# Two feed-forwards opened in another order: block sums ahead of scaled blocks, the seventh operand's low part last

## What is computed

```python
# first block
h2 = rmsnorm(x, norm_ffn[l])
gate, up = jnp.split(h2 @ w_ffn_in[l], 2, axis=-1)
x = x + (jax.nn.silu(gate) * up) @ w_ffn_out[l]
...
# second block
m = rmsnorm_2(x, norm_pre_mlp[l])
y = jnp.square(jax.nn.relu(m @ w_up[l])) @ w_down[l]
x = x + rmsnorm_2(y, norm_post_mlp[l])
```

## Time and profile before

| what | us |
|---|---|
| median of 3 runs | 2688.08 (2687.24 to 2689.71) |
| the profiled execution, its own time | 2686.19 |
| its span | 2684.5 |
| TensorE busy | 2594.2 (97%) |
| VectorE busy | 1859.6 (69%) |
| GpSimd busy | 1222.8 (46%) |
| ScalarE busy | 1042.5 (39%) |

### The profile page before, as it was taken

How to read it: one execution, slowest core, us unless ns; L and a number is a source line. 1 busy time by engine, 2 the same in 40 slices (tenths; PEclk the granted TensorE clock), 3 DMA queues, 4 the chain that set the end, 5 groups by cost and what they waited for, 6 DMA issues and landing times.

```text
span 2684.5 us, 32398 instructions
## 1 busy us (share of the span) xinstructions
PE 2594.2 (97%) x12362; PEld 2088.1 (78%) x12362; DVE 1859.6 (69%) x2107; ACT 1042.5 (39%) x1446; POOL 1222.8 (46%) x763
## 2 busy tenths in 40 slices
PE   7999999999999999999998999989898999999998
PEld 5888787887787888887786788656786888877777
DVE  7565665457658666668879647766558666778887
ACT  5223343323224333334435111656555433434444
POOL 2222222223447888884333443241135888723331
PEclk9999999999999999999999999999999999999999
DMA  5333333244342434245641442401333554754443
GB/s 193 118 103 114 122 94 126 79 157 145 129 145 61 118 102 118 76 133 200 223 130 55 142 149 98 122 1 46 128 85 95 164 160 142 225 158 159 159 141 142
DMA packets 335840, 339.49 MB, mean 126 GB/s; under 512 B 19723, under 2 KB 254838, under 8 KB 335686
## 3 DMA queue, kind: packets, MB, share of 16 engines
q1 hardware_dynamic: 329446, 313.81, 37.2%
q10 hardware_dynamic: 6240, 23.59, 2.2%
HBM read 228.55 MB, written 107.77 MB: 125 GB/s over the span
## 4 chain that ended last, share of the span: by engine, by line
PE 54%; DVE 9%; issue 2%; DMA 2%; ACT 1%; POOL 0%; SPq 0%; DVEq 0%; ACTq 0%; POOLq 0%
PE ps L3729 37%; PE ps L567 9%; PE ps L2787 2%; DVE op_lo L3806 2%; PE ps L2810 1%; PE ps L2797 1%; DVE sw_lo L3625 1%; PE ps L3291 1%; DVE acc L4052 1%; DVE acc L4059 1%; DMA x_block<-acc 0%; DVE acc L2313 0%; DMA acc<-x_feature_major 0%; DVE x L2734 0%; DMA op_raw<-hidden 0%
## 5 line engine op out<-in xcount | busy, mean ns | idle before, releaser
L3729 PE MATMUL ps<-op_hi,sw_hi 128*128 128x512 f32 x1765 | 690.3, 391 | 16.4 <-DVE op_lo L3806 6.5
L3729 PE MATMUL ps<-op_hi,sw_lo 128*128 128x512 f32 x1765 | 686.9, 389 | 0.0
L3729 PE MATMUL ps<-op_lo,sw_hi 128*128 128x512 f32 x1765 | 686.8, 389 | 0.0
L3729 PEld LDWEIGHTS ps<-op_hi,sw_hi 128*128 128x128 f32 x1765 | 331.3, 188 | 97.6 <-issue 16.5
L3729 PEld LDWEIGHTS ps<-op_hi,sw_lo 128*128 128x128 f32 x1765 | 331.3, 188 | 69.5
L3729 PEld LDWEIGHTS ps<-op_lo,sw_hi 128*128 128x128 f32 x1765 | 331.4, 188 | 67.7 <-issue 0.5
L533 POOL TENSOR_TENSOR w_hi_t<-w_raw,ones 128x1024 fp32r<-128x1024 f32 (+1 forms) x60 | 116.1, 1940 | 532.7 <-DMA w_raw<-in_w_in 238.7
L3615 ACT ACTIVATE sw_hi<-sw_sumNone 128x512 fp32r<-128x512 f32 (+1 forms) x252 | 157.0, 624 | 329.6 <-PE ps L3729 237.8
L3625 POOL TENSOR_TENSOR sw_lo<-sw_sumNone,sw_hi 128x512 fp32r<-128x512 f32 x138 | 215.0, 1568 | 33.2 <-ACT sw_hi L3615 33.1
L3576 POOL TENSOR_TENSOR sw_sumNone<-sw_raw 128x512 f32<-128x512 f32 (+1 forms) x63 | 114.2, 1813 | 225.6 <-DVE sw_lo L3625 204.1
L3615 ACT ACTIVATE sw_hi<-sw_raw 128x512 fp32r<-128x512 f32 (+1 forms) x188 | 116.8, 622 | 199.6 <-PE ps L3729 198.3
(11 more groups left out here) (502 smaller groups left out, 5433.2 us busy)
## 6 DMA issues: line engine op xcount, KB each, us to landing
op_raw<-hidden SPq DMA_DIRECT2D x42, 1024.0 KB, 8.8
w_raw<-in_w_in SPq DMA_DIRECT2D x47, 512.0 KB, 4.6
sw_raw<-in_w_ffn_in SPq DMA_DIRECT2D x44, 512.0 KB, 5.1
hidden<-hidden_blocks SPq DMA_DIRECT2D x13, 1536.0 KB, 6.1
hidden<-hidden_blocks SPq DMA_DIRECT2D x14, 1280.0 KB, 5.0
sw_raw<-in_w_up SPq DMA_DIRECT2D x32, 512.0 KB, 8.4
sw_raw<-in_w_down SPq DMA_DIRECT2D x32, 512.0 KB, 5.5
acc<-proj SPq DMA_DIRECT2D x30, 512.0 KB, 4.5
```

The costliest lines, as they stand in the source:

```text
L3729: mm = pe.matmul(out, w, x[:, k, :], start=(k == 0 and i == 0 and r < 4), stop=(k == n - 1 and i == 2), skip_group_check=r >= 4)
```

## The change

In the first opening, DVE makes y_lo of tile 0 only, then the sum "22" of pair 0, then the other three y_lo, then u3 and "22" of pair 1, and only then the scaled blocks; `gate_post` and `up_post` no longer make these two sums. `product` lets (0,6) wait for y_lo tile by tile. In the second opening, operand 6 is parted last instead of first: ACT's high parts go 1, 2, 3, 5, 6, DVE makes the low part of 1 where that of 6 was, and that of 6 behind u3 of pair P2+1.

```diff
-PARTED = (6, 1, 2, 3, 5)
+PARTED = (1, 2, 3, 5, 6)
...
-POSTS = [(0, "u2"), (1, "u2"), (0, "u3"), (0, "22"), (1, "u3")]
-POSTS += [(p, what) for p in range(2) for what in OUTS_OF_PAIR[2 + (p == 0):]]
+POSTS = [(0, "u2"), (1, "u2"), (0, "u3"), (0, "22"), (1, "u3"), (1, "22")]
+POSTS += [(p, what) for p in range(2) for what in OUTS_OF_PAIR[3:]]
...
 # gate_post
-            post_sum(dve, p, what, hidden(i, n))
+            if (p, what) != (0, "22"):
+                post_sum(dve, p, what, hidden(i, n))
...
 # up_post
-            post_sum(dve, p, what, hidden(i, x))
+            if (p, what) != (1, "22"):
+                post_sum(dve, p, what, hidden(i, x))
...
 # f1_dve
-            for k in range(4):
+            y_lo(dve, 0)
+            dve.wait_ge(*count("t_lo", 16))
+            dve.wait_ge(*count("b_lo", 9))
+            post_sum(dve, 0, "22", hidden(0, 6))
+            for k in range(1, 4):
                 y_lo(dve, k)
             for k in (KT - 2, KT - 1):
                 x1_spilled(dve, k)
-            dve.wait_ge(*count("t_lo", 16))
+            post_u3(dve, 1)
             dve.wait_ge(*count("b_lo", 12))
+            post_sum(dve, 1, "22", hidden(0, 1))
             dve.wait_ge(S["rstd_ready"], NORM_AT["ffn"] + 1)
             gate_post(dve, 0, "22")
-            post_u3(dve, 1)
...
 # wo2_act
-            parted_hi(act, 6)
+            parted_hi(act, 1)
             norm_root(act, "mlp", rstd2[:, :])
...
 # product
-            operand_ready(pe, p, r)
+            if (p, r) != (0, 6):
+                operand_ready(pe, p, r)
...
             for k in range(n):
+                if (p, r) == (0, 6):
+                    pe.wait_ge(*count("b_lo", KT + k + 1))
...
 # f2_act
-            parted_hi(act, 1)
...
             parted_hi(act, 5)
+            parted_hi(act, 6)
...
 # hidden_dve
-                parted_lo(dve, 6)
+                parted_lo(dve, 1)
             next_lo(dve, p, 1)
             post_u3(dve, p)
+            if q == 1:
+                parted_lo(dve, 6)
             if q:
                 mix2_dve(dve, q - 1, (2, 3))
             else:
-                parted_lo(dve, 1)
                 dve.wait_ge(S["rstd_ready"], NORM_AT["mlp"] + 1)
```

## The result

The changed kernel takes **2691.6 us** (median of 20 runs, 2688.88 to 2694.3), the kernel before 2687.8 us beside it (20 runs): a ratio of 1.0014, 95% interval 1.0008 to 1.0021. So it is 3.8 us slower, inside the 0.2% that the forecast called no change. The forecast was 2693.3 us, its range 2689.0 to 2696.6. Its profiled execution took 2691.47 us, span 2688.5, against 2686.19 and 2684.5: 5.3 us more by its own time, 4.0 by the span.

What follows compares the result with a forecast made beforehand. TensorE, busy 97%, was taken as the bound, its waits set by VectorE's full queue and turns with GpSimd. First opening 1.1, second 1.3 and clock 2.8 summed to +5.2 us on 2688.08: 2693.3 us, range 2689.0 to 2696.6.

Steps and rivals of the forecast that it cites:

- (a): First opening: with only one y_lo ahead of pair 0's "22", (0,6) starts at 849.4, a gain of 1.4 us.
- (c): First opening: scaling of pair 0's "22" begins 2.0 us later, delaying sw_lo(13); (1,6) still starts at 856.06, gaining 2.9 us.
- (d): First opening: GpSimd's four turns of 1.7 us behind sw_lo(13) make (2,0) start at 862.9, costing +1.1 us.
- (e): Second opening: block sums and operands 2, 3, 5 move 3.4 us forward; (P2+1,3) and (P2+1,5) start sooner, 2.1 us gained.
- (f): Second opening: "22" stands behind operand 6, and VectorE waits one more GpSimd turn; (P2+1,6) comes later, costing +1.3 us.
- The clock: Behind the two new long waits, one in each opening, the granted clock falls once of the two, costing +2.8 us.
- the row of 3.94: Before 22.94 in the old profile: a 3.94 us wait, then 5.6 us of matmuls at half speed, 2.8 us lost.
- Rival B: Both openings: both new waits lower the clock, +8.0 us in all, 2696.1 us; chance 0.22.
- D: Both openings: turns with GpSimd fall out better, -0.6 and -0.5 us, no long wait, 2687.0 us; chance 0.11.
- E: Both openings: the waits simply go, GpSimd being no bound; 7.9 us gained, 2680.2 us; chance 0.05.
- C: Both openings: neither new wait lowers the clock, +2.4 us, 2690.5 us; chance 0.24.

Runs made afterwards that it cites:

- e3: The changed kernel with sw_hi(13) moved ahead of the SiLU of pair 0's "22" on ScalarE; 2686.7 us in one execution.
- e4: The changed kernel with a PSUM bank replacing one SBUF operand in the second gate scaling and gate-up products of pairs 0 and 1; 2689.9 us in one execution.
- e2: The first opening of the kernel before with the changed kernel's second opening; 2690.3 us, ratio 1.0012 to the kernel before.
- e6: The changed kernel with VectorE's "22" of pair P2+1 put ahead of operand 6's low part and other work; 2689.0 us, ratio 1.0008 to the kernel before.
- e1: The changed kernel's first opening with the second opening of the kernel before; 2690.6 us, ratio 1.0009 to the kernel before.
- e10: The kernel before with nine unread matmuls ahead of (1,6); 2684.4 us, ratio 0.9990 to the kernel before.
- e5: e3 with pair 2's weights fetched one product sooner; 2687.6 us in one execution.
- e7: e5 and e6 in one kernel; 2686.4 us, ratio 0.9998 to the kernel before.
- e9: e10 with the second opening of e6 and 12 unread matmuls ahead of (P2+2,0); 2684.5 us, ratio 0.9993 to the kernel before.
- e11: e7 with the mixes of pairs 0 and 1 behind u3 and "22" of pair 2, and 12 unread matmuls ahead of (P2+2,0); 2684.2 us, ratio 0.9991.
- e8: The changed kernel with 14 unread matmuls ahead of (2,0) and of (P2+1,6); 2686.0 us, ratio 0.9998 to the kernel before.

## Why the prediction was right

The chains of the two openings were seen rightly. That the time came within 1.7 us of the forecast is in part luck: structure and clock together came to 1.1 us more than forecast, and something that the sum did not have took 2.5 off again. By its own steps:

- **(a)** (0,6) at 849.4: measured 849.21. Its wait by tiles was used: it stood 0.43 us inside. The turns fell on y_lo(1) and (2) (3.52 us for two) and not on (2) and (3), with the same sum.
- **(c)** The scaling of "22" of pair 0 at 852.8, 2.0 us later: measured 853.06, 2.2 us. The chain behind it was as said. sw_lo(13) was put at 854.7 to 856.0, at 1.30 alone; it began at 855.01 and took 1.79, since a scaling of VectorE met it too. This is the mis-sized part: 0.8 us at the end of sw_lo(13), 856.80. (1,6), put at 856.06, started at 856.90 for it.
- **(d)** Four turns of 1.7 behind it: predicted 6.9 us, measured 856.76 to 863.54, 6.8. (2,0) at 862.9 (+1.1) was therefore 863.64, **+1.9**, beyond the end of +1.6 that was given. e3 confirms the chain, e4 the turns.
- **(e)** (P2+1,5) at +19.1 from (P2,5): measured +19.00.
- **(f)** +1.3: measured **+1.04**. The two op_lo went from 5.58 to 6.69, the 1.1 us of the one further turn. e2 shows the same alone. That VectorE's unchanged sum of work had to hold (P2+1,6) was true only of this order: e6 has it 5.5 us sooner, and the bound is then GpSimd, which (f) called no bound.
- **The clock.** +2.8 as one fall of the two: the sum is near, the mechanism not. The clock fell behind both waits, in this profile and in every other one that has them unfilled, and cost 1.7 us each time, 3.4 together, less than the 2.8 taken from the row of 3.94; only e1 paid 2.8 for one. Rival B had the number of falls right and, but for e1, their size wrong; the forecast's "one fall of the two" was wrong.
- **What the sum left out** is that the kernel it is measured against pays for its own wait of 2.3 to 2.6 us. Its profile showed 1.00 there, and was taken for the rule. Structure 1.9 + 1.0 and clock 3.4 make 6.3 us; the medians differ by 3.8. The 2.9 us that e10 takes off the kernel before, if they are all clock, bring it to 3.4; e10's interval allows 0.3 to 5. That the forecast's +5.2 is near the difference of the two profiled executions (5.3; 4.0 by the span) is chance, for the clock in stretches that no edit touches differs by as much. By the same rule, a low clock behind the wait of 2.12 us at 1716 to 1719 took 5.1 us in the profile before and 3.4 in the one after; behind one of 6.5 us at 1466 to 1469 again 5.1 and 3.4; behind one of 1.90 us at 1889 nothing before and 1.7 after. Together that is 10.2 us before and 8.5 after, though not all of it is lost time, since TensorE also rests in these stretches.
- **Rivals.** D and E fell: GpSimd's operations were all at 1.61 to 1.79, and the scaling ended at 853.74, not before 852.2. C fell, since the clock fell both times; its 2690.5 is near the median only because it leaves out both the falls and what the kernel before pays.

Open stays how often the kernel before falls at (1,6): profiles show single executions, and of the waits of 2.1 to 2.6 us here two lowered the clock (e2, e4) and four did not (before, e3, and e5 and e7 at (2,5)).

## What to carry to other kernels

Where an in-order engine is full, moving one sum forward moves a wait. Follow what the displaced operation feeds through every engine behind it, and then further than the first gain: in e5, e7, e9 and, in its second opening, e11 the gain at one product was spent waiting at the next bound (VectorE's u3; weights that landed late). Several short waits can cost less than one long one of the same sum: in these two openings the clock fell only behind waits of over 2.5 us. Where such a wait can't be removed, matmuls that nobody reads, kept shorter than the wait, kept the clock up here (e8; 4.3 us by the ratios) and moved the start behind them by 0.0 to 0.3 us. And a profile of the kernel before is one execution: read its clock at each wait as a sample.

## What the hardware showed

- In the two openings the granted clock fell behind waits of 2.85 to 3.76 us in all ten places where a profile has one; behind those of 2.1 to 2.6 us in two of six; behind those of 1.5 us and less in none. TensorE was at full work on both sides. The falls began between 1.2 us ahead of the wait's end (e1) and 0.8 us behind it (the changed kernel, second opening). Ten of the twelve cost 1.7 us each, the other two 2.8 (e1) and 2.9 (e2).
- Length alone does not settle it: elsewhere, where TensorE also rests between shorter pieces of work, the clock fell behind a wait of 2.12 us in all 14 profiles (at about 1716) and behind one of about 1.9 us in 11 of 14 (at about 1889).
- A 128x512 operation on GpSimd takes 1.27 to 1.30 us alone and 1.6 to 1.8 against a VectorE operation with two SBUF operands; a PSUM operand on VectorE's side in place of one of them takes the difference away (e4).
- e3 and e5 have the same list on VectorE, but in e5 GpSimd starts on pair 2 sooner. VectorE's u3 of pair 2 then came 28.4 us behind (0,5) (874.45 - 846.08), in e3 27.4 (873.43 - 846.07): feeding GpSimd sooner put a full VectorE 1.0 us back, which fits the turns that the two take, though no run isolates it.
- The releaser that a row names can be wrong by one: (2,0)'s named a VectorE operation that ended 0.02 us behind GpSimd's sw_lo.
